# Two weight rings moved to 1024-byte boundaries in on-chip memory

## What is computed

```
u = rmsnorm(h);  proj = u @ w_in                # 528 tokens
o = [neighbourhood attention, gated linear attention]
h = h + rmsnorm(o @ w_o)
a = conv3(rmsnorm(h) @ w_ffn_in);  h = h + rmsnorm((gelu(gate) * val) @ w_ffn_out)
x = h[16:]                                      # 512 tokens, second block
proj = modulate(rmsnorm(x)) @ w_in_2
x = x + g_m * (merge(sparse attention, depthwise conv) @ w_out_2)
x = x + g_f * ((silu(a) * b) @ w_ffn_out_2), with a, b = modulate(rmsnorm(x)) @ w_ffn_in_2
return rmsnorm(x)
```

## Time and profile before

| | |
|---|---|
| median of three runs | 1462.42 us (1462.09 to 1462.65) |
| span of the profiled execution | 1461.6 us, 21126 instructions |
| TensorE matmuls | busy 1432.6 us, 98% of the span, 8882 matmuls |
| TensorE weight loads | busy 1235.6 us, 85%, 8882 |
| VectorE, ScalarE, GpSimd | 810.1, 556.9, 535.9 us |
| mean granted TensorE clock | 0.996 of 2.4 GHz |

### The profile page before, as it was taken

The page is one execution under the profiler, slowest core; times in us unless marked ns, Lnnn a source line. Parts: engine busy times, 40 slices in busy tenths (PEclk is TensorE's granted clock), DMA queues, the critical chain, the costliest instruction groups (busy, mean ns, idle before and its releaser), DMA issues.

```text
span 1461.6 us, 21126 instructions
## 1 busy us (share of the span) xinstructions
PE 1432.6 (98%) x8882; PEld 1235.6 (85%) x8882; DVE 810.1 (55%) x1155; ACT 556.9 (38%) x879; POOL 535.9 (37%) x227
## 2 busy tenths in 40 slices
PE   9999999999999999999999999999999999999997
PEld 8988787999999999888788767678888888888887
DVE  6832645346666666455799789863453343432123
ACT  6432434453222233232523364455344333333221
POOL 1421111224434434444244323224434444544441
PEclk9999999999999999999999999999999999999999
DMA  7210221113223224876232212212223233323332
GB/s 252 89 59 30 72 71 44 59 59 94 95 87 101 88 88 156 297 279 231 87 102 90 87 59 86 72 44 87 89 84 130 101 130 113 131 89 100 102 114 87
DMA packets 44829, 154.75 MB, mean 106 GB/s; under 512 B 4992, under 2 KB 7808, under 8 KB 44736
## 3 DMA queue, kind: packets, MB, share of 16 engines
q1 hardware_dynamic: 44080, 150.79, 30.7%
q10 hardware_dynamic: 656, 2.62, 0.6%
HBM read 151.17 MB, written 2.10 MB: 105 GB/s over the span
## 4 chain that ended last, share of the span: by engine, by line
PE 76%; DVE 6%; ACT 1%; issue 1%; DVEq 0%; ACTq 0%
PE G L523 71%; DVE scb L2300 1%; DVE small L2298 1%; PE B L1098 1%; PE B L1122 1%; PE B L1070 1%; DVE G L1792 1%; PE G L1109 0%; PE B L493 0%; DVE xlo L1800 0%; DVE S L2351 0%; DVE B L2347 0%; PE G L812 0%; DVE G L2241 0%; DVE small L2354 0%
## 5 line engine op out<-in xcount | busy, mean ns | idle before, releaser
L448 POOL TENSOR_TENSOR wlo<-raw,whi 128x1024 fp32r<-128x1024 f32 x222 | 535.4, 2414 | 902.7 <-ACT whi L1214 902.7
L1214 ACT ACTIVATE whi<-raw 128x1024 fp32r<-128x1024 f32 x225 | 237.5, 1056 | 280.8 <-DMA raw<-wstream 170.5
L523 PE MATMUL G<-xhi,whi 128*128 128x512 f32 (+1 forms) x692 | 273.7, 396 | 2.0 <-DVE xlo L1800 1.8
L523 PE MATMUL G<-xhi,wlo 128*128 128x512 f32 (+1 forms) x692 | 267.5, 387 | 0.0
L523 PE MATMUL G<-xlo,whi 128*128 128x512 f32 (+1 forms) x692 | 267.2, 386 | 0.0
L523 PE MATMUL G<-uhi,whi 128*128 128x258 f32 (+3 forms) x1200 | 251.2, 290 | 8.2 <-DVE vT L1942 2.5
L523 PE MATMUL G<-uhi,wlo 128*128 128x258 f32 (+3 forms) x1200 | 244.3, 284 | 0.0
L523 PE MATMUL G<-ulo,whi 128*128 128x258 f32 (+3 forms) x1200 | 243.4, 283 | 0.0
L523 PEld LDWEIGHTS G<-uhi,whi 128*128 128x128 f32 x1200 | 186.9, 191 | 21.2 <-issue 15.7
L523 PEld LDWEIGHTS G<-uhi,wlo 128*128 128x128 f32 x1200 | 186.7, 190 | 0.0
L523 PEld LDWEIGHTS G<-ulo,whi 128*128 128x128 f32 x1200 | 186.4, 190 | 0.0
(11 more groups left out here) (348 smaller groups left out, 1676.0 us busy)
## 6 DMA issues: line engine op xcount, KB each, us to landing
raw<-wstream SPq DMA_DIRECT2D x225, 512.0 KB, 3.4
ada_in<-ada SPq DMA_DIRECT2D x40, 512.0 KB, 6.1
ada_late<-ada SPq DMA_DIRECT2D x8, 512.0 KB, 3.5
h<-hT SPq DMA_DIRECT2D x8, 264.0 KB, 3.4
out<-res SPq DMA_DIRECT2D x8, 256.0 KB, 2.2
biasn<-bias SPq DMA_DIRECT2D x2, 960.0 KB, 8.0
biasn<-bias ACTq DMA_DIRECT2D x2, 960.0 KB, 4.7
scan_keep<-scanm SPq DMA_DIRECT2D x1, 528.0 KB, 7.4
```

The source lines that it names most:

```text
L448: pool.tensor_tensor(wlo[:, i, :], raw[:, i, :], whi[:, i, :].bitcast(F32), ALU.subtract)\
L523: ins = pe.matmul(dst[:, x, 0:xw], w[:, slot, b * P:(b + 1) * P], u[:, k, off + x0:off + x0 + xw], start=(first and i == 0 and j == 0), st ...
L1214: act.activation(whi[:, m % RING, :], raw[:, m % RING, :], ACT.Copy).then_inc(s["unit_hi"], 1)
```

## The change

Two roundings of the running address are put in: one ahead of the rings, and the one ahead of the large area goes from 64 to 1024.

```
         xhi = sb("xhi", [P, KD, SEQ], U_AT + 512, F32R)
         xlo = sb("xlo", [P, KD, SEQ], U_AT + 512 + KD * SEQ * 4, F32R)
+        at = -(-at // 1024) * 1024
         raw = sb("raw", [P, RING, BLK * P], at)
...
         small = sb("small", [P, 160], at); at += 640
-        A0 = -(-at // 64) * 64
+        A0 = -(-at // 1024) * 1024
```

## The result

The changed kernel takes 1486.66 us (1483.57 to 1489.17) against 1462.54 us, the median of the kernel before with a fourth run of 1465.79 added. It is slower, by a ratio of 1.0154, 95% interval 1.0138 to 1.0169; this ratio is estimated from the single runs, and the two medians alone would give 1.0165. The profiled execution has a span of 1486.6 us, 25.0 more than before, at a mean granted clock of 0.997 against 0.996, so that the clock is not the cause. The forecast of no change was wrong; what came is the slower rival.

What follows compares the result with a forecast made beforehand. The prediction took TensorE, busy 98% of the span, with line 523's ring matmuls, as the bound. Its terms, 1461.6 + 0 + 0 + 0 + 0 us of span and 0.8 us around it, gave 1462.4 us, range 1450 to 1489.

Steps and rivals of the forecast that it cites:

- forecast of no change: Whole kernel: no measurable change, 1462.4 us, with a range of its own of 1459.5 to 1465.3; chance 0.45.
- slower rival: Line 523: weights and moving rows 128 bytes apart cost 3 ns on each of 7320 intervals, 1484.4 us; chance 0.32.
- I take 0: Ring weights as read by TensorE: their new addresses cost 0, with ends of -10.5 and 22.0 us.
- upper end of that step: Ring weights as read by TensorE: 3 ns a matmul, taken from `ones_r`, on 7320 matmuls, 22.0 us.
- Fact 1: Ring matmuls: shifts by 256, 512 and 1024 bytes between weights and moving rows do nothing.
- Fact 2: Ring matmuls: small shifts (8, 32, 48 bytes) do little; excess 10.0 and 11.7 ns against 13.3 for level rows.
- Fact 3: Only `ones_r` shows an offset of 128: four matmuls take 0.50 us against 0.48 with `ups`, 2.5 to 5 ns each.
- faster rivals: Ring matmuls lose excess: in part, 1451.9 us, chance 0.20; by much, 1390.6 us, chance 0.03.
- rival that was faster by much: Ring matmuls: excess falls to the 2.6 ns of the `ones` rows, 71.8 us less, 1390.6 us; chance 0.03.
- terms taken as zero: Fillers' raw, wlo, whi; vec, ident, ones, small; large area: cost 0 each, the small tensors at worst 4.7 us.

Runs made afterwards that it cites:

- e2_r256: The rings alone moved up by 256 bytes against the kernel before: ratio 1.0007.
- e2_r128: The rings alone moved up by 128 bytes against the kernel before: ratio 1.0169.
- e1_small_only: Rings kept; vec, ident, ones and small moved up by 384 bytes and the large area by 1024, against the kernel before: ratio 0.9995.
- e2_r32: The rings alone moved up by 32 bytes against the kernel before: ratio 1.0157.
- e3_u32: Rings kept; uhi and ulo begin 32 columns (128 bytes) further into their padded rows, against the kernel before: ratio 1.0022.
- e1_rings_only: The rings alone moved up by 384 bytes, as in the change, against the kernel before: ratio 1.0150.
- e2_x_back: The rings moved up by 384 bytes, and xhi and xlo by 384 with them, against the kernel before: ratio 1.0085.

## Why the prediction was wrong

*The step that failed* is the last of the change's parts, "I take 0" for the ring weights as read by TensorE. It measured 24.1 us. The bound was right (TensorE, line 523), and the upper end of that step, 22.0 us by `ones_r`, was near; the choice between the ends was not. The runs show in its place that the interval depends on the distance between weight block and moving row, by 256 bytes: 226.9 ns where the two stand level, 232.6 where the change put them.

*Fact 1* held: 256, 512 and 1024 bytes change nothing (e2_r256, 1.0007). But it says only that the cost repeats by 256; it says nothing of what lies between, and there the change moved.

*Fact 2* carried the choice, and it failed twice. It read the ffn_in rows as starting 48 bytes off. They do not: that stage writes its rows from column 0 (line 1531 of the kernel before) and reads them there, so its 258-wide halves begin level and 8 off. The rows that do start 48 off are those of w_o (from column 12, lines 885 and 908), which the prediction did not read. There 24 intervals take 2.88 us, 120.0 ns each:

```profile
275.06 0.40 PE L523 MATMUL G<-uhi,whi 128*128 128x258 f32 x2
...
277.94 0.40 PE L523 MATMUL G<-uhi,whi 128*128 128x258 f32 x2
```

So at this width 48 and 56 bytes off do cost little, but every ring row off level was narrow, 256 to 264 columns. And narrow rows can't stand for wide ones: at 64 bytes 256-wide intervals fell from 120.0 to 113.8 ns while the 512-wide ones rose from 226.9 to 233.6. The trace of before had no 512-wide matmul off level at all, and so no row that could have said zero.

*Fact 3* pointed the right way. `ones_r` gave 2.5 to 5 ns for 264 columns, from four matmuls; the change cost 3.3 ns there, 4.1 at 258 in the profiled run and 5.7 at 512 columns. It was set aside because thousands of intervals spoke against it, but those thousands were level or narrow. That its size came near is in part luck: in nanoseconds the four intervals are 118, 130, 118 and 127, so that they swing by more than the price.

*The slower rival* had the cause, the distance between weights and moving rows, and very nearly the sum, 1484.4 us against 1486.66, but "the same growth in all four widths" is wrong. 512 columns pay most, and 256 columns gain 1.7 ns. That 3 ns on all 7320 came out near the mean of these, 24.1 us / 7320 = 3.3, is luck. The wide matmuls alone make 5.7 ns x 3288 = 18.7 us, as an estimate (the prediction counted 3096 and left out 192 of ch, cl, ah and al). And the piece that begins in ffn_in grew by 9.58 us in the profiled run of the change, but by 2.59 in e2_r128, at the same distance.

*The faster rivals.* That level rows have the largest excess was no sign that wide matmuls pay for being level: at 512 columns level is the cheapest of the seven places tried. For 256 columns the idea held, 118.3 ns in the change and 113.8 at 64 bytes, but these are few. The price of the rival that was faster by much comes from the `ones` rows, and there a reading was off: line 1016 runs 16 matmuls and leaves 32 records, so that the sixteen of the earlier trace rows are eight float32 matmuls of two records each, and 216 ns is the time of a record.

*The terms taken as zero* for the fillers, the small tensors and the large area were right: e1_small_only has 0.9995, and GpSimd's 2414 ns, ScalarE's 1055 and the load's 3.3 us stand within a nanosecond or a tenth of a us of before.

*Why the distance counts* is open. At 264 columns the price shows at the clock's upper level, 2.4 GHz (123.3 against 120.0 ns), and not at the lower one, 1.2 GHz: with 0.50 granted sixteen matmuls of the changed kernel, now 128 off, take 3.52 us, 220 ns each, as they did level. The timeline of PE and the window there:

```profile
10.66 0.64 PE L524 MATMUL G<-uhi,whi 128*128 128x264 f32 x2
...
14.18 0.64 PE L578 MATMUL G<-uhi,whi 128*128 128x264 f32 x2
```

```profile
10.70:14.40 3.70, 3.70 (x19) 3.70 (x18) 3.70 (x6) 3.70 (x7) 0.00 (x0) 0.50 0.89 272
```

At the upper level moving either operand changes the interval: the rings by 32 bytes, 226.9 to 233.6 ns at 512 columns (e2_r32); u by 128, 119 to 121 ns at 258 (e3_u32). The Trainium skill, "TensorE: Matmul & The Clock Gate", section "Step-by-step: what each phase is for", has weights loaded without taking read bandwidth from the running matmul. Read so that no distance between the two could cost anything, it does not agree with these runs. That the two reads meet in the memory, and that level rows let them pass by one another, is argued from the dependence on the pair and from the price that is not there at half clock; no run shows it. Why 192 bytes cost a third of what 160 and 224 do is open too.

## What to carry to other kernels

Where float32r matmuls with a weight load ahead of each set the time, choose the addresses of the weight blocks and the moving rows as a pair, and check the start-to-start interval in the timeline: here a distance that is a multiple of 256 bytes gave 226.9 ns for 512 columns and of the six others tried five gave 232.6 to 233.6. Measure at the width that sets the time, since 256 columns went the other way. Pad rows and rings so that the distance holds for every block, and move both or neither. And before a row is taken as evidence of no effect, work out whether it ever stood in the other condition.

## What the runs showed of the hardware that was not expected

The same distance can have more than one pace, and a pace holds for a whole stage. At 128 bytes the piece that begins in ffn_in took 310.49 us in the changed kernel and in e1_rings_only, but 303.50 us in e2_r128 and 303.51 us in e2_x_back, which stand to u by the same distance by 256. That is 7.0 us between programs whose first-block addresses differ by a multiple of 256 or, between e1_rings_only and e2_x_back, not at all; e3_u32 had a third pace, 304.26 us. One run of each program was traced, so that a change of pace between two runs of one program is not shown. It would fit the spread of their times: e2_r128 took 1480.51 us in the profiled run and up to 1490.80 in the others, 10.3 us apart, where the kernel before, over 18 runs on one chip, stayed within 5.3 us. Which pace a run takes was not found out.

A block off level slows its neighbours: with whi alone moved the wide interval was 235.42 / 1008 = 233.6 ns on the average of all three products, as high as with both rings moved by 32, 64, 160 or 224 bytes. And the same distance can cost one width and pay another: 64 bytes cost 512 columns 6.7 ns and gave 256 columns 6.2.
